# Twenty more transposing jobs of a two-block transformer step move from TensorE to VectorE's 32x32 squares and on-chip transfers

## The chip, the cores and the metric

One core of one Trainium2 chip runs the whole program. The metric is the device time of one execution in microseconds (us). Lower is better.

## What is computed

The reference runs three layers one after the other on 256 tokens of width 2048, all in float32: a pooling mixer, a sparse attention whose keys an indexer picks, and a block with an mLSTM branch, a MoBA attention branch and a feed-forward part. Almost all of the work is in products of the tokens with weight matrices. Between them stand norms, rotations and attention.

```
h = rms_norm(x, g) * (1 + scale) + shift              # twice, one per mixer
out = (mixed * silu(gate)) @ w_out                    # pooling
q, k, v, gate, qi, ki, wi = split(h @ w_in)           # q, k: 8 blocks of 512 columns
out = (sparse_attention(rope(q), rope(k), v, picked by qi, ki, wi) * silu(gate)) @ w_out
x = rms_norm(x + gate * out, final_g)
mq, mk, mv, mo, mi, mf, aq, ak, av, g_m, g_a = split(rmsnorm(x, w) @ w_in_2)
mq, mk = silu(causal_depthwise_conv([mq, mk], 4 taps))
merged = sigmoid(g_m) * (h_m @ w_m) + sigmoid(g_a) * (h_a @ w_a)
x = x + rmsnorm(merged @ w_out_2);   x = x + rmsnorm(relu(norm(x) @ w_up)**2 @ w_down)
```

## The kernel before, in words

**The product.** Everything that is multiplied by weights goes through one pipeline. A weight matrix of 2048 rows is read in *blocks* of 512 columns, and each block in 8 *chunks* of 256 rows (512 KB). SyncE loads a chunk into one of 8 buffers `raw`. ScalarE rounds it to the short float32r form (`hi`, L524), VectorE subtracts that from the original (`lo`, L1057), and TensorE then multiplies in three passes, so that the sum has nearly the precision of float32: tokens-hi by weights-hi, tokens-hi by weights-lo, tokens-lo by weights-hi (L1924 to L1926). A chunk is 12 matmuls of 128x512. `w_hi` and `w_lo` have 4 buffers each, so ScalarE can start on chunk n only when TensorE is through with chunk n-4, and the two engines run at most about three chunks ahead. How long a chunk's `lo` is finished before TensorE starts it is called its *lead* here.

**The order of the work** is written out by hand for each engine. `blk` walks over the chunks from 3 to 10 (0 to 2 of the next block included), and *hooks* hang other work behind a chunk: `{5: f}` runs `f` after chunk 5 of this walk, `{2: f}` before the first of it. At the end of a block ScalarE empties PSUM into `stage` (`evac`, L536 and L532), and VectorE does there what the block needs (rotations of q and k, gating, residual sums). Nothing lets an engine run its own list in another order.

**The transposing jobs.** The products have tokens on the partitions, but the next product or the attention needs features there. So a block's 256 tokens by 512 features in `stage` are transposed. TensorE does this in a *job*: 8 transposes of 128x128 (L1994) into two PSUM banks, hung behind chunk 3 of the next block. VectorE then takes the result out of PSUM (`leave`, L1139 and L1141, hook 5), ScalarE rounds it to `hi` where it is the token side of a product (`split`, L563), and VectorE subtracts (`low_part`, L1149). The 4 causal taps of the convolution (`conv`, L1594 and L1597, hooks 7 to 10) read their job's PSUM banks directly.

**The other way** exists already in the feed-forward part. There VectorE transposes the 32x32 squares of `stage` into `blocks` in one instruction (L1845), GpSimd issues 16 transfers of 32 partitions by 1 KB each, from SBUF to SBUF, which bring the squares to their partitions in `gathered` (L510), and ScalarE and VectorE take them from there (L989). A transposed block with its 16 transfers is called a *turn* below, its 16 transfers a *cross*, and the instruction that reads `gathered` the *taker*.

**Stages** in order, with their blocks of weights: `qk` (8 blocks), `gate` (4), `v` (4), attention, `attn_out` (4), `m_qk` (4), `m_v` (2), `m_o` (2), mLSTM, `a_qk` (4), `a_v` (2), MoBA, `g_m` (4), `g_a` (4), `branch` (4), `mix_out` (4), feed-forward (32). In `gate`, *riders* go along: VectorE adds up 512 KB pieces of `mod_w` beside the weights (L1300), one for each chunk, with a load of their own each. The jobs are named after the stage or norm they serve: `qk` (8), `norm2` (4, in `attn_out`), `m_qk` (4), `a_qk` (4), `branch` (4). The last job of one stage falls in the first block of the next. Between `m_qk` and `m_v` stands `m_if`, a product of 8 columns, whose result TensorE transposes back in `if_back` (L2292), behind chunk 0 of the second block of `m_v`.

GpSimd's queue also carries the large transfers: the residual to DRAM and back (2 MB each), the rows that are spread over all partitions (`final_g`, `gate_row` and others, 1 MB each). It works in order.

## Time and profile before

| | us |
|---|---|
| median of 3 runs (2375.24 to 2379.03) | 2377.76 |
| the profiled execution | 2376.75 |
| its span, first to last instruction | 2374.9 |
| TensorE busy (98%) | 2326.1 |
| VectorE busy (64%) | 1528.7 |
| ScalarE busy (47%) | 1117.7 |
| GpSimd busy (6%) | 140.4 |
| one block of 96 matmuls without anything between them | 21.76 |

Execution time and span differ by what lies around the first and last instruction. Matmuls are pipelined in the profile, so the starts of two of them, and not their durations, tell how long TensorE needs for one. A busy share is an average over stages that differ: what a change is worth is read where it stands, from which wait ends last.

### The profile page before, as it was taken

The page shows a single profiled execution, that of the slowest core. Times are in us where ns is not written, and L with a number is a line of the kernel's source. Part 1 is how long each engine was busy: PE and PEld are TensorE (multiplying, and loading weights), DVE is VectorE, ACT ScalarE, POOL GpSimd, SP SyncE. Part 2 cuts the span into 40 slices and gives each one's busy share as a digit, 9 for nine tenths or more (in the row PEclk, how much of TensorE's full clock was granted, in tenths as well). Part 3 has the DMA queues.
Part 4 walks back from the last instruction along what each step waited for, and adds up shares of the span by engine and source line. Part 5 has one row for each costly group of instructions (what it writes and reads, how often), then busy time and mean ns, then how long its engine had stood idle before and what let it go on. Part 6 is the DMA issues. An engine that isn't in the chain of part 4 may idle for free.

```text
span 2374.9 us, 30018 instructions
## 1 busy us (share of the span) xinstructions
PE 2326.1 (98%) x10902; PEld 1888.6 (80%) x10902; DVE 1528.7 (64%) x1863; ACT 1117.7 (47%) x1347; POOL 140.4 (6%) x277
## 2 busy tenths in 40 slices
PE   5999999999999999999999999999999999999998
PEld 1877777888788878888888888888888888888886
DVE  2988887666697556875765444665665665565566
ACT  1444445444444455545444444454554444454454
POOL 0000000000000000000000000000131121121120
PEclk8999999999999999999999999999999999999999
DMA  9999996555597546656454766556566666666663
GB/s 392 386 377 378 376 398 250 181 178 176 191 382 268 169 157 196 224 160 188 133 185 151 238 193 190 179 198 196 177 213 208 201 211 204 203 209 195 209 208 110
DMA packets 253414, 536.59 MB, mean 226 GB/s; under 512 B 25068, under 2 KB 25332, under 8 KB 249336
## 3 DMA queue, kind: packets, MB, share of 16 engines
q1 hardware_dynamic: 241520, 510.40, 63.6%
q0 software_dynamic: 10128, 22.07, 2.7%
q10 hardware_dynamic: 1656, 2.65, 0.3%
q8 instruction: 69, 1.13, 0.2%
q14 instruction: 41, 0.34, 0.0%
HBM read 520.35 MB, written 6.30 MB: 222 GB/s over the span
## 4 chain that ended last, share of the span: by engine, by line
PE 93%; DVE 3%; DMA 2%; ACT 1%; issue 1%; ACTq 0%; DVEq 0%; SPq 0%
PE ps L1924 29%; PE ps L1926 29%; PE ps L1925 29%; PE ps L1994 2%; DMA ifb<-in_f_bias 1%; PE ps L2024 1%; PE ps L2203 0%; DMA T<-in_mod_w 0%; DVE w_lo L1057 0%; PE ps L2244 0%; PE ps L2103 0%; PE ps L2180 0%; ACT tmp L807 0%; PE ps L2246 0%; PE ps L2245 0%
## 5 line engine op out<-in xcount | busy, mean ns | idle before, releaser
L1057 DVE TENSOR_TENSOR w_lo<-raw,w_hi 128x1024 fp32r<-128x1024 f32 x784 | 944.9, 1217 | 527.9 <-ACT w_hi L524 513.5
L524 ACT CAST w_hi<-raw 128x1024 fp32r<-128x1024 f32 x784 | 815.7, 1046 | 875.0 <-PE ps L1926 827.5
L1924 PE MATMUL ps<-w_hi,xa_hi 128*128 128x512 f32 x2176 | 855.4, 393 | 5.3 <-DVE w_lo L1057 3.1
L1926 PE MATMUL ps<-w_hi,xa_lo 128*128 128x512 f32 x2176 | 847.5, 389 | 0.0
L1925 PE MATMUL ps<-w_lo,xa_hi 128*128 128x512 f32 x2176 | 846.9, 389 | 0.0
L1924 PEld LDWEIGHTS ps<-w_hi,xa_hi 128*128 128x128 f32 x2176 | 408.6, 188 | 99.5 <-issue 11.0
L1926 PEld LDWEIGHTS ps<-w_hi,xa_lo 128*128 128x128 f32 x2176 | 408.5, 188 | 85.9
L1925 PEld LDWEIGHTS ps<-w_lo,xa_hi 128*128 128x128 f32 x2176 | 408.7, 188 | 82.6
L1924 PE MATMUL ps<-w_hi,xb_hi 128*128 128x512 f32 x928 | 364.6, 393 | 2.0 <-issue 1.3
L1926 PE MATMUL ps<-w_hi,xb_lo 128*128 128x512 f32 x928 | 361.4, 389 | 0.0
L1925 PE MATMUL ps<-w_lo,xb_hi 128*128 128x512 f32 x928 | 361.2, 389 | 0.0
L1924 PEld LDWEIGHTS ps<-w_hi,xb_hi 128*128 128x128 f32 x928 | 174.2, 188 | 45.9 <-issue 9.2
L1926 PEld LDWEIGHTS ps<-w_hi,xb_lo 128*128 128x128 f32 x928 | 174.2, 188 | 36.5
L1925 PEld LDWEIGHTS ps<-w_lo,xb_hi 128*128 128x128 f32 x928 | 174.3, 188 | 35.2
L510 POOL DMA_DIRECT2D T<-T x256 | 125.2, 497 | 512.8 <-DVE T L1845 451.8
L536 ACT ACTIVATE stage<-ps 128x1024 f32<-128x1024 f32 (+1 forms) x60 | 61.6, 1026 | 85.9 <-PE ps L1926 85.9
L1300 DVE SCALAR_TENSOR_TENSOR T<-T,csil 128x1024 f32<-128x1024 f32 x64 | 81.9, 1280 | 9.3 <-DMA T<-in_mod_w 7.4
L1300 DVE SCALAR_TENSOR_TENSOR wide<-T,csil,wide 128x1024 f32<-128x1024 f32 x64 | 81.9, 1279 | 0.5 <-DVE stage L1236 0.4
L2024 PE MATMUL ps<-T,csil 128*32 128x256 f32 (+1 forms) x384 | 45.4, 549 | 21.2 <-DMA T<-in_mod_w 21.1
L1880 DVE TENSOR_TENSOR T<-T,stage 128x1024 f32<-128x1024 f32 x27 | 33.1, 1225 | 32.6 <-ACT stage L536 32.5
L2024 PEld LDWEIGHTS ps<-T,csil 128*32 128x32 f32 x384 | 8.1, 114 | 48.4 <-DMA T<-in_mod_w 27.2
L1139 DVE COPY T<-ps 128x1024 f32 (+1 forms) x14 | 17.1, 1224 | 40.2 <-PE ps L1994 40.2
(266 smaller groups left out, 1046.9 us busy)
## 6 DMA issues: line engine op xcount, KB each, us to landing
raw<-in_w_in SPq DMA_DIRECT2D x176, 512.0 KB, 3.9
T<-in_mod_w SPq DMA_DIRECT2D x160, 512.0 KB, 7.7
raw<-in_attn_w_in SPq DMA_DIRECT2D x144, 512.0 KB, 4.5
raw<-in_w_up SPq DMA_DIRECT2D x128, 512.0 KB, 4.2
raw<-in_w_down SPq DMA_DIRECT2D x128, 512.0 KB, 4.5
raw<-in_pool_w_in SPq DMA_DIRECT2D x64, 512.0 KB, 8.0
T<-in_mod_w SPq DMA_DIRECT2D x16, 1024.0 KB, 8.9
raw<-in_pool_w_out SPq DMA_DIRECT2D x32, 512.0 KB, 8.9
```

What stands on the lines that cost most here:

```text
L510: pool.dma_start(gathered[32 * f:32 * f + 32, a, :, :], blocks[32 * a:32 * a + 32, f, :, :]).then_inc(blocks_landed, 16)
L524: nc.scalar.copy(w_hi[:, o % SPL, :, 0:cols], raw[:, o % RAW, :, 0:cols]).then_inc(hi_ready, 1)
L536: nc.scalar.activation(dst, ps[:, bass.ds((A % 2) * 2, 2), :], func).then_inc(acc_free, 1)
L1057: tt(w_lo[:, o % SPL, :, part], raw[:, o % RAW, :, part], w_hi[:, o % SPL, :, part].bitcast(F32), ALU.subtract).then_inc(lo_ready, 1)
L1139: nc.vector.tensor_copy(dst, src).then_inc(tp_evac, 1)
L1300: stt(acc, ride_raw[:, o % 4, :], csil[:, bass.ds(b * 4 + o // 2, 1)], acc, ALU.mult, ALU.add).then_inc(mod_used, 1)
L1880: tt(y, y, stage[:], ALU.add).then_inc(combined, 1)
L1924: mm(dst, x_hi, h, start=first and k == 0, stop=False)
L1925: mm(dst, x_hi, l, start=False, stop=False)
L1926: ins = mm(dst, x_lo, h, start=False, stop=last and k == KPC - 1)
L1994: ins = nc.tensor.transpose(dst, part, ident)
L2024: ins = mm(ps[32 * q:32 * q + 32, bank, at:at + n], col, src[:, q * n:q * n + n], start=first, stop=k == KC - 1, skip_group_check=True)
```

## The change

Twenty of TensorE's jobs become turns: 8 of `qk`, 3 of `norm2`, 2 of `m_qk` (blocks 0 and 1 of its 4), 4 of `a_qk`, 3 of `branch`. The last job of `norm2` and of `branch`, and the last two of `m_qk`, stay on TensorE. The table of jobs is cut, and a table of turns is new:

```diff
-        ("idx_kw", 2, False), ("qk", 8, False), ("attn", 4, True), ("norm2", 4, True), ("m_qk", 4, False), ("m_if", 1, False),
-        ("mlstm", 2, True), ("a_qk", 4, False), ("moba", 2, True), ("branch", 4, True), ("norm3", 4, True),
+        ("idx_kw", 2, False), ("qk", 0, False), ("attn", 4, True), ("norm2", 1, True), ("m_qk", 2, False), ("m_if", 1, False),
+        ("mlstm", 2, True), ("a_qk", 0, False), ("moba", 2, True), ("branch", 1, True), ("norm3", 4, True),
...
+    for name, jobs in (("qk", 8), ("norm2", 3), ("m_qk", 2), ("a_qk", 4), ("branch", 3)):
```

GpSimd gets the crosses, between its large transfers. From the second turn of a group on, a cross also waits until the taker before it has read `gathered`:

```diff
+            def cross(src, dst, landed):
+                for a in range(4):
+                    for f in range(4):
+                        pool.dma_start(dst[32 * f:32 * f + 32, a, :, :], src[32 * a:32 * a + 32, f, :, :]).then_inc(landed, 16)
+            def turns(name, jobs, src, dst, taken, first=0):
+                for b in range(jobs):
+                    pool.wait_ge(turn_ready, TURNS[name] + b + 1)
+                    if b:
+                        pool.wait_ge(taken, first + b)
+                    cross(src, dst, turn_landed)
...
+            turns("qk", 8, blocks, gathered, unfolded)
...
             widen(gate_row)
+            turns("norm2", 3, blocks, gathered, xh_ready, SPLITS["norm2"])
             pool.wait_ge(res_done, 1)
             pool.dma_start(tokens(resid[1]), T2[:]).then_inc(res_stored, 16)
+            turns("m_qk", 2, blocks3, gathered3, unfolded, 8)
+            turns("a_qk", 4, blocks3, gathered3, unfolded, 10)
...
+            turns("branch", 3, blocks, gathered, x_ready, SPLITS["branch"])
```

VectorE's transpose, and the places where it stands. In `qk` it follows the rotation, ahead of the next block's first `lo`; in `norm2` it stands behind chunk 3; in `m_qk` ahead of chunk 3; in `a_qk` where `leave` stood; in `branch` ahead of chunk 3:

```diff
+            def turn_blocks(dst, done):
+                nc.vector.transpose(dst.rearrange("p f q i -> p q f i"),
+                                    stage[:].rearrange("p t (f c i) -> p (t f) c i", c=4, i=32)).then_inc(done, 1)
+            def turn(name, b, dst):
+                if TURNS[name] or not (isinstance(b, int) and b == 0):
+                    dve.wait_ge(turn_landed, b * 256 + TURNS[name] * 256)
+                turn_blocks(dst, turn_ready)
...
-                blk(b + B0, {3: lambda: qi_out_now(b), 5: lambda: qk_out(b - 1), 9: lambda: index_scores(b)})
+                blk(b + B0, {3: lambda: qi_out_now(b), 9: lambda: index_scores(b)})
                 query_key(b, b + A0)
+                qk_turn(b)
...
-            phase("gate", first={5: lambda: qk_out(7)})
+            phase("gate")
...
+            with step.loop(2, n, 2) as b:
+                blk(b + B0, {3: lambda: norm_turn(b - 1), 5: lambda: norm_low(b - 2)})
...
-                blk(b + B0, {7 + f: (lambda f=f: conv(b - 1, f)) for f in range(4)})
+                blk(b + B0, {1: {2: lambda: conv_turn(0)}, 2: {2: lambda: conv_turn(1), **convs(0, 3)},
+                             3: {**convs(1, 3), **convs(2, 7)}}[b])
...
             def aqk_out(b):
-                leave(b + JOBS["a_qk"], feat(2)[:, bass.ds(b * 4, 4), :])
+                turn("a_qk", b, blocks3)
...
+                if not first:
+                    dve.wait_ge(staged, b + STAGED["branch"])
+                    turn("branch", b - 1, blocks)
```

The takers are ScalarE's, each one block later than the job's `leave` was. `unfold` copies `gathered` to where the attention or the convolution reads it. `norm2_split` scales four strips by the norm's weights into `tmp` and rounds them; `split_gathered` only rounds:

```diff
+            def unfold(name, b, src, dst):
+                act.wait_ge(*turned(name, b))
+                nc.scalar.copy(dst.rearrange("p f (t a i) -> p f t a i", t=NT, a=4),
+                               src.rearrange("p a (t f) i -> p f t a i", t=NT)).then_inc(unfolded, 1)
...
+            with act.Fori(2, n) as b:
+                blk(b + B0, {2: lambda: qk_unfold(b - 2), 8: lambda: index_relu(b)})
...
+                blk(B0 + b, {2: lambda: qk_unfold(6 + b)} if b < 2 else None)
...
+                blk(B0 + b, {**({2: lambda: norm2_split(b - 2)} if b > 1 else {}), 6: lambda: attn_squares(b - 1)})
...
+                    {}, {2: lambda: conv_unfold(0), 8: lambda: conv_silu(0)},
+                    {2: lambda: conv_unfold(1), 7: lambda: conv_silu(1)})):
...
+                blk(B0 + b, {4: lambda: aqk_unfold(b - 2)} if b > 1 else None)
...
+                    if o == 3 and not isinstance(b, int):
+                        split_gathered(*turned("branch", b - 2), XB, b - 2)
```

TensorE loses the jobs. The two convolution jobs that stay use one PSUM bank pair, which `if_back` uses too, so its wait now covers the last of the convolutions:

```diff
-                blk(b + B0, b + A0, XB, True, {3: lambda: qk_job(b - 1), 5: lambda: index_scores(b)})
-            phase("gate", XB, first={3: lambda: qk_job(7)})
+                blk(b + B0, b + A0, XB, True, {5: lambda: index_scores(b)})
+            phase("gate", XB)
...
+            def conv_job(b):
+                job(b + (JOBS["m_qk"] - 2), stage, acc_free, PHASES["m_qk"][1] + b + 1, bank=4)
...
             def if_back():
                 pe.wait_ge(acc_free, PHASES["m_if"][1] + 1)
-                pe.wait_ge(tp_evac, JOBS["m_if"] - 1)
+                pe.wait_ge(tp_evac, JOBS["m_if"])
```

How VectorE's instructions stand at two places. First, the end of the last `qk` block and the start of `gate`, before (`COPY stage<-tmp` ends the rotation, `wide<-T,csil,wide` is a rider, `w_lo` is the `lo` of a chunk, `T<-ps` is `leave`):

```order
L1236 COPY stage<-tmp 128x8x16 [waits dve_step]
L167 REGISTER_ALU
L173 REGISTER_ALU [waits dve_step]
L173 COMPARE_AND_BRANCH
L1300 SCALAR_TENSOR_TENSOR wide<-T,csil,wide 128x1024 [waits ride_landed0,bias_landed]
L1300 SCALAR_TENSOR_TENSOR wide<-T,csil,wide 128x1024 [waits ride_landed1,mod_used]
L1300 SCALAR_TENSOR_TENSOR wide<-T,csil,wide 128x1024 [waits ride_landed2,mod_used]
L1057 TENSOR_TENSOR w_lo<-raw,w_hi 128x1024 [waits hi_ready,mod_used]
```

and now:

```order
L1353 COPY stage<-tmp 128x8x16 [waits dve_step]
L180 REGISTER_ALU
L1256 STREAM_TRANSPOSE T<-stage 128x8x4x32 [waits dve_step,turn_landed]
L186 REGISTER_ALU
L186 COMPARE_AND_BRANCH
L1417 SCALAR_TENSOR_TENSOR wide<-T,csil,wide 128x1024 [waits ride_landed0,bias_landed]
L1417 SCALAR_TENSOR_TENSOR wide<-T,csil,wide 128x1024 [waits ride_landed1,mod_used]
L1417 SCALAR_TENSOR_TENSOR wide<-T,csil,wide 128x1024 [waits ride_landed2,mod_used]
L1158 TENSOR_TENSOR w_lo<-raw,w_hi 128x1024 [waits hi_ready,mod_used]
```

The transpose has come between the rotation and the three riders that stand ahead of chunk 3 of `gate`; the `leave` two chunks further on is gone.

Second, the end of block 0 of `m_qk` and the start of its block 1, before (`T<-T,small` is the first output of a token tile, `if_lo` the low part of the gates' weights):

```order
L1578 SCALAR_TENSOR_TENSOR T<-T,small 128x2048
L1057 TENSOR_TENSOR w_lo<-raw,w_hi 128x1024 [waits hi_ready,dve_step]
L1578 SCALAR_TENSOR_TENSOR T<-T,small 128x2048
L1605 TENSOR_TENSOR if_lo<-if_raw,if_hi 128x128 [waits dve_step,if_high]
L1057 TENSOR_TENSOR w_lo<-raw,w_hi 128x1024 [waits hi_ready] x5
L1594 TENSOR_SCALAR tmp<-ps,vec 128x256 [waits tp_ready]
L1597 SCALAR_TENSOR_TENSOR tmp<-ps,vec,tmp 128x253 [waits dve_step]
```

and now:

```order
L1709 SCALAR_TENSOR_TENSOR T<-T,small 128x2048
L1158 TENSOR_TENSOR w_lo<-raw,w_hi 128x1024 [waits hi_ready,dve_step]
L1709 SCALAR_TENSOR_TENSOR T<-T,small 128x2048
L1746 TENSOR_TENSOR if_lo<-if_raw,if_hi 128x128 [waits dve_step,if_high]
L1256 STREAM_TRANSPOSE T<-stage 128x8x4x32 [waits turn_landed,acc_free]
L1158 TENSOR_TENSOR w_lo<-raw,w_hi 128x1024 [waits hi_ready] x8
L1256 STREAM_TRANSPOSE T<-stage 128x8x4x32 [waits turn_landed,acc_free]
```

A transpose has come ahead of chunk 3 of block 1, and the first convolution has left that block: it stands in block 2, behind the second transpose.

## Rows read from the trace of the kernel before

**Rows 1.** The page, busy time of each engine, and the chain that ended last.
```profile
PE 2326.1 (98%) x10902; PEld 1888.6 (80%) x10902; DVE 1528.7 (64%) x1863; ACT 1117.7 (47%) x1347; POOL 140.4 (6%) x277
...
PE 93%; DVE 3%; DMA 2%; ACT 1%; issue 1%; ACTq 0%; DVEq 0%; SPq 0%
```

**Rows 2.** Timeline of TensorE at a `qk` job: start us, duration us, instruction.
```profile
510.51 0.39 PE L1926 MATMUL ps<-w_hi,xa_lo 128*128 128x512 f32 x1
510.74 1.03 PE L1994 MATMUL ps<-con,stage 128*128 128x128 f32 x8
511.53 0.48 PE L1924 MATMUL ps<-w_hi,xa_hi 128*128 128x512 f32 x1
```

**Rows 3.** Groups by form: busy us, mean ns of one | idle before.
```profile
L1845 DVE STREAM_TRANSPOSE T<-stage 128x1024 f32<-128x1024 f32 x16 | 19.9, 1246 | 0.5
...
L989 ACT CAST xa_hi<-T 128x1024 fp32r<-128x1024 f32 x16 | 16.8, 1049 | 9.5 <-DMA T<-T 9.5
...
L1139 DVE COPY T<-ps 128x1024 f32 x10 | 12.2, 1224 | 33.2 <-PE ps L1994 33.2
```

**Rows 4.** Timeline of VectorE in block 3 of `qk`: `lo` of chunk 3.
```profile
527.85 1.23 DVE L1057 TENSOR_TENSOR w_lo<-raw,w_hi 128x1024 fp32r<-128x1024 f32 x1 [0.65 <-ACT w_hi L524]
```

**Rows 5.** TensorE starting chunk 3 (`qk` 3, `gate` 0, `attn_out` 3, `m_qk` 1), then `if_back`.
```profile
531.76 0.39 PE L1924 MATMUL ps<-w_hi,xa_hi 128*128 128x512 f32 x1
...
651.68 0.50 PE L1924 MATMUL ps<-w_hi,xa_hi 128*128 128x512 f32 x1 [0.93 <-DVE w_lo L1057]
...
932.81 0.39 PE L1924 MATMUL ps<-w_hi,xb_hi 128*128 128x512 f32 x1
...
978.15 0.39 PE L1924 MATMUL ps<-w_hi,xa_hi 128*128 128x512 f32 x1
...
1069.06 0.29 PE L2292 MATMUL ps<-con,stage 8*128 8x8 f32 x2
```

**Rows 6.** Timeline of VectorE at the start of `gate`.
```profile
646.44 3.93 DVE L1300 SCALAR_TENSOR_TENSOR wide<-T,csil,wide 128x1024 f32<-128x1024 f32 x3 [0.39 <-DVE stage L1236]
650.40 1.22 DVE L1057 TENSOR_TENSOR w_lo<-raw,w_hi 128x1024 fp32r<-128x1024 f32 x1
```

**Rows 7.** Timeline of VectorE where block 1 of `m_qk` begins.
```profile
976.51 0.29 DVE L1605 TENSOR_TENSOR if_lo<-if_raw,if_hi 128x128 fp32r<-128x128 f32 x1 [0.16 <-DVE T L1578]
976.72 4.62 DVE L1057 TENSOR_TENSOR w_lo<-raw,w_hi 128x1024 fp32r<-128x1024 f32 x4
```

**Rows 8.** Timeline of VectorE in `m_v`: the last taps of the last convolution.
```profile
1068.38 1.52 DVE L1597 SCALAR_TENSOR_TENSOR tmp<-ps,vec,tmp 128x253 f32<-128x253 f32 x3
```

**Rows 9.** Timelines of ScalarE (end of a block) and VectorE in `attn_out` 3.
```profile
925.01 1.03 ACT L536 ACTIVATE stage<-ps 128x1024 f32 x1 [1.83 <-PE ps L1926]
...
930.04 3.49 DVE L1057 TENSOR_TENSOR w_lo<-raw,w_hi 128x1024 fp32r<-128x1024 f32 x3
```

**Rows 10.** Crosses of the feed-forward part: VectorE, GpSimd and ScalarE timelines, GpSimd's waits.
```profile
1735.53 1.25 DVE L1845 STREAM_TRANSPOSE T<-stage 128x1024 f32<-128x1024 f32 x1
...
1747.98 2.93 POOL L510 DMA_DIRECT2D T<-T  x6 [5.85 <-issue]
...
1824.08 7.82 POOL L510 DMA_DIRECT2D T<-T  x16 [51.21 <-DVE T L1845]
...
1754.24 1.05 ACT L989 CAST xa_hi<-T 128x1024 fp32r<-128x1024 f32 x1 [1.26 <-DMA T<-T]
...
POOL T L510 <- issue: 60.9, 13, 6.3
```

**Rows 11.** Stretches of 23 and 22 us in `qk` and `gate`: ..., clock, DMA share, GB/s.
```profile
476.00:499.00 23.00, 23.00 (x111) 18.66 (x110) 15.83 (x25) 10.18 (x12) 0.00 (x0) 1.00 0.57 186
...
666.00:688.00 22.00, 22.00 (x99) 18.23 (x98) 20.93 (x19) 9.72 (x10) 0.00 (x0) 1.00 1.02 385
```

**Rows 12.** Timelines of GpSimd and VectorE around the start of `attn_out`.
```profile
872.97 0.54 POOL L465 DMA_DIRECT2D wide<-gate_row  x1 [11.93 <-DMA T<-in_final_g]
...
881.23 1.22 DVE L1377 TENSOR_TENSOR stage<-stage,wide 128x1024 f32<-128x1024 f32 x1 [2.08 <-DMA wide<-gate_row]
```

More of the change, by code:

```diff
@@ L126, in _jobs @@
         JOBS[name], SPLITS[name] = n, s
-        n, s = n + jobs, s + (4 if name == "shift0" else jobs if split else 0)
+        n, s = n + jobs, s + (4 if name in ("shift0", "norm2", "branch") else jobs if split else 0)
 _jobs()
@@ L507, in _ @@
                 pool.wait_ge(blocks_ready, n + 1)
[L508 to L511 removed]
+                cross(blocks, gathered, blocks_landed)
         @block.scalar
@@ L1774, in _ @@
             branch(0, first=True)
-            with step.loop(1, n, 2) as b:
+            branch(1)
+            with step.loop(2, n, 2) as b:
                 branch(b)
@@ L2351, in _, with branch @@
             B0, A0, n = PHASES["branch"]
[L2352 to L2354 removed]
+            def branch(b):
                 for half in range(2):
```

228 lines of the change are left out of this document (139 added, 89 removed).

## The prediction, made before the changed kernel ran

> **What bounds the kernel now.** I read four views, in this order. The page says which engine ends the program: TensorE is busy for 98% of the span, and 93% of the chain that ended last is TensorE's own work; the other engines have a third to a half of their time free on average [rows 1]. So every TensorE instruction that goes away shortens the program, as long as what replaces it arrives in time on engines with room. The timeline of TensorE gives the price of a job. The job's first transpose starts at 510.74 in the ordinary step of 0.23 us behind the last product, and the next product starts at 511.53 [rows 2]. A job costs 0.79 us.
>
> The average hides where the other engines have no room. The place that matters is chunk 3 of each block: ScalarE's emptying of PSUM and VectorE's end-of-block work both stand ahead of it, while TensorE has only three finished chunks, 8.2 us, to live on. So the third view is that chunk's lead, VectorE's timeline against TensorE's. It is 531.76 - 529.08 = 2.7 us in the middle of `qk` [rows 4, 5]. In block 1 of `m_qk` it is 0.2: the first of four `lo` that begin at 976.72 ends near 977.95, TensorE starts at 978.15 [rows 5, 7]. At the start of `gate` there is none, TensorE already idles 0.93 us for it [rows 5, 6]. The fourth view is how long a cross takes, read in the feed-forward part.
>
> **The change part by part.**
>
> *TensorE.* Twenty jobs at 0.79 us leave: **-15.8 us**. All stood behind chunk 3 of a block full of products, and nothing but products moves up.
>
> *VectorE.* Each turn is one transpose of 1.25 us where `leave` took 1.22 [rows 3]. The amount is the same; the place is not.
> - `qk`: `leave` stood at hook 5, the transpose stands ahead of chunk 3. It takes 1.25 of a lead of 2.7 and leaves 1.4. Cost 0; in block 1, where the engine came late from the indexer's first block, I allow 0 to 0.3.
> - `gate`, block 0: the same transpose stands ahead of three riders that together take 3.93 us and a `lo` that TensorE already waits for [rows 5, 6]. Everything is in series there: **+1.2**.
> - `m_qk`, block 1: the transpose stands ahead of the `lo` with a lead of 0.2 [rows 7]. 1.25 - 0.2: **+1.0**. The engine runs without a break there, so nothing absorbs it. The convolutions that move to blocks 2 and 3 make VectorE lose 0.55 us a chunk against TensorE (1.22 for `lo` and about 2.05 for a strip, against 2.72), over four and then eight chunks. They start from some 3 us of lead, and the eight-column product of `m_if` gives 5.5 us back behind them: 0, at most 1.
> - `attn_out`, `a_qk`, `branch`: the transpose is off the path. In `a_qk` it stands exactly where `leave` did; in `branch` it takes 1.25 of some 3 us of lead.
>
> *`if_back`.* It now waits for the last taps of the last convolution. They end at 1068.38 + 1.52 = 1069.90 [rows 8], and the transposes started at 1069.06 [rows 5]: 0.84 and a semaphore, **+0.9**.
>
> *ScalarE* gets 14 copies that it did not have, 1.05 us each [rows 3]. The three takers of `branch` replace a `split` of the same size; those of `norm2` grow from 1.05 to about 3.0 (four quarter strips of about 0.5 in front). With 8 `hi` and an emptying it uses about 10 of 23 us a block in `qk` [rows 11], so the work fits. What matters is when the cross has landed, since ScalarE, and every `hi` behind it, stands still until then. The shortest possible cross is 16 issues in 7.82 us and some 4 us more; but GpSimd often pauses in the middle, 5.85 us in one case, 13 times in 256 issues [rows 10]. So most crosses hold a pause. A paused one ran from the transpose's end at 1736.78 to its taker at 1754.24, 17.5 us, and ScalarE waited 1.26 for it [rows 10].
> - `qk`: the block of rows 4 starts at 531.76 - 8.16 = 523.6, and the transpose would end 4.9 us into it. A block will last 22.95 us, and ScalarE has emptied it 1.4 us after its end (926.04 in a block that starts at 932.81 - 8.16 = 924.65 [rows 5, 9]). From transpose to taker there are 19.4 us; ScalarE has 1.4 us more before it delays VectorE, and the lead is 1.4: safe up to 22 us. Cost 0.
> - `norm2`: the `lo` begins at 930.04, the transpose follows and ends near 932.5. ScalarE is free for the taker when it has emptied the next block, 21.76 us after 926.04 [rows 9], so 15.3 us later. A cross of 17.5 makes it 2.2 late. Then 3.0 for the taker, 1.05 for `hi` and 1.2 for `lo` end 7.45 after the emptying, at 933.5 in this block's frame, and TensorE wants the chunk at 932.81 [rows 5]: 0.7 late. Only a pause near the end of a cross does this. I count one of three: **+0.7**, 0 to 2.1.
> - `m_qk`, `a_qk`, `branch`: the takers are up to 2.5 us late as well, but at hooks 3 and 4, or with 2 us in hand: 0.
>
> *GpSimd and the transfers.* 320 issues at 0.49 us are 157 us in a queue that is busy for 6% now. A cross moves 0.5 MB beside a weight stream that uses 57% of the DMA engines in `qk`: room. In `gate` the share is 1.02, 385 GB/s [rows 11], and the last cross of `qk` falls there: 0 to 1.4 us if the loads have to make way (0.5 MB at that rate). I take 0, since the lead grows through that stage and the removed `leave` gives VectorE 1.2 back.
>
> **Sum:** -15.8 + 1.2 + 1.0 + 0.9 + 0.7 = -12.0. The profiled execution took 2376.75 and the median of the runs is 1.0 above it, so 2377.76 - 12.0 = **2366 us**. Below 0.2% (4.8 us) a measurement of this kernel can hardly tell a difference from none.
>
> **The rivals.**
>
> *A, everything hidden.* No transpose and no taker costs TensorE anything; then it is 2377.8 - 15.8 = 2362. For it: the large leads in most blocks. Against it: three of the four costs stand in unbroken series in the trace. Chance 0.09.
>
> *B, crosses held up by large transfers and full DMA engines.* If a pause means that GpSimd waits for whatever is under way, it is longer behind a large transfer. `gate_row` took from 872.97 to about 881.2, and VectorE idled 2.08 us for it [rows 12]; were the load ahead of it held up by the reload of the residual, the first residual sum would be 1 to 3 us later, with a lead of 1.4 there. The first cross of `m_qk` comes right behind a store of 2 MB. With `gate` slowed by up to 1.4, this adds 1 to 5 us: 2369. Chance 0.15. The Trainium skill ("DMA: Bandwidth & Descriptors", the section on the descriptor swizzle) counts 9 descriptors per DMA engine for a 128-partition transfer of 1 MiB, 8 of data and one of completion. By that count a transfer of 32 partitions needs 3, and the pauses would come from a full list of descriptors, at places that the large transfers shift; the trace fits in that unpaused and paused crosses alternate irregularly, and no row shows a pause behind a large transfer.
>
> *C, the freed time comes back as waits.* If the next chunk 3 were VectorE's to decide in most stages, TensorE would wait there for what it saved. In `a_qk` it already waits about 0.1 us a block. But that wait is measured from the start of a block, and the job stood behind the chunk, so it doesn't grow. The result would be within 5 us of before: 2374. Chance 0.07.
>
> *D, slower: crosses that take 20 us.* The windows are 15.3 us plus 1.5 of lead in `norm2`, about 18 in `a_qk`, 22 in `qk`. At 20 us each, `norm2` loses 3 x 3.2, `a_qk` 4 x 1.8, `branch` and `m_qk` some 3 more: 2366 + 19 = 2385. It is slower than before from about 19 us on. For it: the longest of the feed-forward part is 17.5, only 1.5 less, and there the taker stands 16 us behind the transpose. Against it: the 16 issues take 0.49 us each, evenly, while VectorE works beside them [rows 10], and these stages load the DMA engines no more than that one does. Chance 0.05, with all other causes of a slower run. The Trainium skill ("SBUF — State Buffer", the section on who interferes with whom) says that GpSimd can't write a transfer's descriptors while VectorE runs a float32 copy inside SBUF: such a transfer goes from some 620 to 3100 ns. The rotations of `qk` and `a_qk` end in such a copy, of 0.2 to 0.4 us. If it held up all 16 issues fivefold, a cross would take over 40 us, by that estimate far slower than before; a single short copy can delay one issue. Of that the feed-forward rows show nothing.
>
> **The numbers.** The sum's way has 0.64, A 0.09, B 0.15, C 0.07, D 0.05. The range goes from A's value less the scatter of a median to B's far end, 2361.5 to 2373. Faster by over 0.2% are the sum, A and B, 0.88; within it is C, 0.07; slower is D, 0.05.
>
> **What would show it.** 160 transposes fewer: TensorE's L1994 group with source `stage` falls from 288 to 128. TensorE's idle at chunk 3 of `gate` 0 grows from 0.93 to about 2.1; a new one of 1.0 stands in `m_qk` 1; `if_back` waits for a convolution for 0.9. In `attn_out` ScalarE waits for a cross before at most two takers, and no other taker delays TensorE. All `qk` blocks get shorter by 0.8. I am wrong if waits of ScalarE for `gathered` stand ahead of waits of TensorE in `qk` or `a_qk`, if `gate` is longer by over 2 us, or if GpSimd's pauses are much longer than 6 us.

## The result, and the profile after

| | before | changed |
|---|---|---|
| median of 4 runs (us) | 2377.49 (2375.24 to 2379.03) | 2363.07 (2362.46 to 2365.53) |
| ratio, 95% interval | | 0.9946 (0.9934 to 0.9958) |
| the profiled execution, its span | 2376.75, 2374.9 | 2362.46, 2360.7 |

The changed kernel is 14.4 us faster, 0.5%; 2366 was predicted, in a range of 2361.5 to 2373. The page of the changed kernel, busy time and chain, against [rows 1]:

```profile
PE 2310.7 (98%) x10742; PEld 1872.0 (79%) x10742; DVE 1531.1 (65%) x1868; ACT 1134.5 (48%) x1373; POOL 297.3 (13%) x597
...
PE 89%; DVE 4%; ACT 2%; DMA 2%; issue 2%; POOL 1%; ACTq 0%; DVEq 0%
```

TensorE lost exactly 160 instructions, 20 jobs of 8. ScalarE and GpSimd took up the takers and the crosses. GpSimd is for the first time in the chain that ended last, with 1%.

**Where the time went, block by block.** A block's length is the time from its first product to the next block's. Not all of the 14.2 us between the two spans is the change's. TensorE's timeline at the first product of `qk`, before and after:

```profile
452.65 0.47 PE L1924 MATMUL ps<-w_hi,xa_hi 128*128 128x512 f32 x1
```

```profile
451.28 0.47 PE L2056 MATMUL ps<-w_hi,xa_hi 128*128 128x512 f32 x1
```

Up to there the change moves no instruction, and the changed run is 1.37 us ahead. The profiles of all runs scatter there, from 451.1 to 453.6 (see e7), so I count this as chance. From there to the end of the span it is 2374.9 - 452.65 = 1922.25 before and 2360.7 - 451.28 = 1909.42 after: **-12.8 us**. The block lengths give the same. A name like `qk` 3 stands for block 3 of that stage, counted from 0:

| blocks | before | changed | difference |
|---|---|---|---|
| 18 blocks that only lost their job | 22.65 to 24.01 each | 21.76 to 23.09 | -16.6 |
| `gate` 0 (lost a job) | 23.88 | 25.45 | +1.6 |
| `m_qk` 0 (keeps its job) | 22.69 | 23.17 | +0.5 |
| `m_qk` 1 (lost a job) | 22.65 | 23.51 | +0.9 |
| `m_v` 1 (`if_back`) | 22.89 | 23.91 | +1.0 |
| all others (mainly a wait in the attention behind `v` 3) | | | -0.2 |

**A job was worth 0.92, not 0.79.** Each of the 18 blocks got shorter by 0.87 to 1.02, most by 0.89 or 0.93. The product behind a job starts 0.79 after the first transpose [rows 2], but the next product starts 0.31 behind that one, where the ordinary step is 0.23. This is its row in the kernel before, behind the last of rows 2 (511.53):

```profile
511.84 0.40 PE L1925 MATMUL ps<-w_lo,xa_hi 128*128 128x512 f32 x1
```

That makes 0.87. The rest, up to 0.06, is in the next few steps, each some ns longer than usual.

**The gate.** VectorE's timeline in the changed kernel, then TensorE's, against [rows 5, 6]:

```profile
638.48 1.25 DVE L1256 STREAM_TRANSPOSE T<-stage 128x1024 f32<-128x1024 f32 x1
639.65 3.88 DVE L1417 SCALAR_TENSOR_TENSOR wide<-T,csil,wide 128x1024 f32<-128x1024 f32 x3
643.57 1.22 DVE L1158 TENSOR_TENSOR w_lo<-raw,w_hi 128x1024 fp32r<-128x1024 f32 x1
```

```profile
644.85 0.50 PE L2056 MATMUL ps<-w_hi,xa_hi 128*128 128x512 f32 x1 [1.80 <-DVE w_lo L1158]
...
645.88 0.45 PE L2057 MATMUL ps<-w_lo,xa_hi 128*128 128x512 f32 x1
646.12 0.63 PE L2058 MATMUL ps<-w_hi,xa_lo 128*128 128x512 f32 x1
...
649.52 0.39 PE L2057 MATMUL ps<-w_lo,xa_hi 128*128 128x512 f32 x1
```

The wait grew from 0.93 to 1.80, as foreseen in kind. The rest was not foreseen: 1.2 us behind the wait, eight steps in a row take 0.43 in place of 0.23. The stretches around it (columns: us, PE, PEld, DVE, ACT and POOL busy, granted clock, DMA share, GB/s) name the cause:

```profile
642.66:644.85 2.19, 0.39 (x3) 0.01 (x1) 2.15 (x3) 1.05 (x1) 2.19 (x5) 1.00 0.96 328
644.85:646.10 1.25, 1.25 (x5) 1.04 (x6) 1.22 (x2) 0.00 (x0) 1.25 (x4) 0.99 0.94 331
646.10:649.50 3.40, 3.40 (x9) 2.63 (x8) 3.37 (x3) 0.10 (x1) 0.77 (x2) 0.50 1.05 342
```

For 3.4 us the granted clock is 0.50, that is 1.2 for 2.4 GHz: 8 x 0.20 = 1.6 us. Gross, with the lost job put back, the block costs 2.5: 0.9 of wait and 1.6 of clock.

**The late cross.** GpSimd's and ScalarE's timelines in `norm2` (second and third turn):

```profile
902.33 2.46 POOL L494 DMA_DIRECT2D T<-T  x5 [12.61 <-DVE T L1256]
909.20 5.37 POOL L494 DMA_DIRECT2D T<-T  x11 [4.41 <-issue]
925.47 4.88 POOL L494 DMA_DIRECT2D T<-T  x10 [10.90 <-DVE T L1256]
935.09 2.94 POOL L494 DMA_DIRECT2D T<-T  x6 [4.74 <-issue]
```

```profile
919.02 1.71 ACT L925 ACTIVATE tmp<-T,vec 128x256 f32<-128x256 f32 x4 [1.30 <-DMA T<-T]
941.21 1.71 ACT L925 ACTIVATE tmp<-T,vec 128x256 f32<-128x256 f32 x4 [1.73 <-DMA T<-T]
```

Two crosses in a row hold a pause of over 4 us. The first makes its taker 1.3 late, so the next transpose comes late as well, and the third taker is 1.7 late. The loss falls in `m_qk` 0 and 1. There TensorE waits for chunk 3 behind the transpose, and in `m_v` for the convolution:

```profile
971.13 0.50 PE L2056 MATMUL ps<-w_hi,xa_hi 128*128 128x512 f32 x1 [1.45 <-DVE w_lo L1158]
...
1061.40 0.25 PE L2423 MATMUL ps<-con,stage 8*128 8x8 f32 x2 [0.98 <-DVEq L1733]
```

### The profile page after: what moved, and what is told of

It reads as the page before. It is cut to its first block, busy times and chain, and to the rows that moved or that the text cites. A ratio compares the mean times of both kernels' runs of the same rounds, so it can differ in the third digit from the quotient of the medians.

```text
span 2360.7 us, 29885 instructions
## 1 busy us (share of the span) xinstructions
PE 2310.7 (98%) x10742; PEld 1872.0 (79%) x10742; DVE 1531.1 (65%) x1868; ACT 1134.5 (48%) x1373; POOL 297.3 (13%) x597
## 4 chain that ended last, share of the span: by engine, by line
PE 89%; DVE 4%; ACT 2%; DMA 2%; issue 2%; POOL 1%; ACTq 0%; DVEq 0%
PE ps L2056 28%; PE ps L2058 28%; PE ps L2057 28%; DMA ifb<-in_f_bias 1%; PE ps L2126 1%; PE ps L2156 1%; DVE w_lo L1158 1%; POOL T L494 1%; PE ps L2335 1%; ACT w_hi L563 0%; DMA T<-T 0%; PE ps L2376 0%; PE ps L2235 0%; PE ps L2312 0%; ACT tmp L880 0%
## 5 line engine op out<-in xcount | busy, mean ns | idle before, releaser
L494 POOL DMA_DIRECT2D T<-T x576 | 282.0, 498 | 1186.0 <-DVE T L1256 1031.0
L1256 DVE STREAM_TRANSPOSE T<-stage 128x1024 f32<-128x1024 f32 x36 | 44.8, 1244 | 3.8 <-ACT stage L571 1.7
```

Source lines behind the costliest of these rows:

```text
L494: pool.dma_start(dst[32 * f:32 * f + 32, a, :, :], src[32 * a:32 * a + 32, f, :, :]).then_inc(landed, 16)
L1256: nc.vector.transpose(dst.rearrange("p f q i -> p q f i"), stage[:].rearrange("p t (f c i) -> p (t f) c i", c=4, i=32)).then_inc(done, 1)
```

## The experiments

Each is the changed kernel with the edit shown, and was profiled once beside the kernel before on the same chip; three were also timed in five runs. A single run's total says little about 1 or 2 us: the head of the program ahead of `qk`, where no instruction is edited, ended at 451.3 in the changed kernel's profile and at 453.0 and 453.4 in those of two variants. Most block lengths repeat to 0.05 us from profile to profile, and they decide. Four don't: `attn_out` 1 and 3 and `m_qk` 0 and 1 vary by up to 0.7 even where nothing in them was edited, so a difference there in a single profile shows little.

### e1_gate_late: the transpose out of the gate's first chunks

```diff
-            with step.loop(1, n, 11) as b:
+            with step.loop(1, n - 1, 11) as b:
...
+            blk(B0 + n - 1, {3: lambda: qi_out_now(n - 1), 9: lambda: index_scores(n - 1)})
+            query_key(n - 1, A0 + n - 1)
...
-            phase("gate")
+            phase("gate", first={5: lambda: qk_turn(7)})
...
-                blk(B0 + b, {2: lambda: qk_unfold(6 + b)} if b < 2 else None)
+                blk(B0 + b, {2: lambda: qk_unfold(6 + b // 2)} if b in (0, 2) else None)
```

> The eighth transpose of qk stands behind chunk 5 of the first gate block, where leave stood before, and its taker in the third gate block. Theory (the transpose in series with the riders makes TensorE wait, and the longer wait sets the clock to half for 3.4 us): block 0 of gate falls from 25.45 us to 22.9 to 23.1, TensorE's wait at chunk 3 from 1.80 to 0.6, and no stretch with a granted clock of half there; the whole 2.5 us shorter. Rival (the clock fell for another reason than the wait): the block falls by 1.2 only, to 24.2, and the half clock stays. Second rival (the cross falls between full DMA engines and is late for the third block): ScalarE waits before its taker there and the third gate block gets longer than 21.76.

Measured: 2360.67. `gate` 0 is 23.13, and no half clock:

```profile
644.68 0.50 PE L2058 MATMUL ps<-w_hi,xa_hi 128*128 128x512 f32 x1 [0.75 <-DVE w_lo L1158]
```

```profile
644.68:648.00 3.32, 3.32 (x15) 2.74 (x16) 3.29 (x3) 0.60 (x2) 0.00 (x0) 1.00 0.92 329
```

The block gets the whole 2.3 back; the third gate block stays at 21.76. Neither rival holds. Not all of it reaches the end, though: the last block of `v` with the attention behind it lasts 57.74 here for 57.45 in the changed kernel, 0.3 more. It does so in all three profiles that have this edit (e1, e7, e10) and in no other of the changed kernel's variants; before it was 57.69. There one wait of TensorE for ScalarE is 1.08 in place of 0.80. Why it depends on this edit isn't shown. The net gain is 2.0.

### e2_gate_warm and e6_warm8: TensorE busy while it waits

The diff is e2's; e6 has 8 for 16.

```diff
+            def warm():
+                for _ in range(16):
+                    mm(ps[:, 5, 0:P], ident, ident, start=True, stop=True)
...
-            phase("gate", XB)
+            phase("gate", XB, first={2: warm})
```

> As the changed kernel, with 16 matmuls of 128x128 into an unused PSUM bank ahead of chunk 3 of the first gate block, which fill about 1.8 us of TensorE's wait there. The sum is the same: no useful work is moved. Theory (idle time of TensorE makes the clock fall): no half clock behind it, the block falls from 25.45 to 23.9 to 24.1. Rival (the clock falls with what VectorE, the transfers or power do there, or on its own): the half clock stays and the block stays at 25.4 or gets longer.

> As e2_gate_warm, with 8 matmuls in place of 16: there one took 0.21 us, so 16 filled 3.5 us where the wait was 2.0, and the 1.5 us too many hid what the clock gave back. Eight end about when chunk 3 is ready. Theory: no half clock behind them, block 0 of gate 23.9 to 24.1 for 25.45 in the changed kernel. Rival (the block is as long whatever TensorE does in the wait): 25.3 or more again.

Measured: 2361.13 and 2363.13. TensorE's timeline of e2, then of e6:

```profile
642.68 3.73 PE L2327 MATMUL ps<-con 128*128 128x128 f32 x32
646.17 0.48 PE L2056 MATMUL ps<-w_hi,xa_hi 128*128 128x512 f32 x1
```

```profile
645.23 1.95 PE L2327 MATMUL ps<-con 128*128 128x128 f32 x16
647.19 0.50 PE L2056 MATMUL ps<-w_hi,xa_hi 128*128 128x512 f32 x1
```

The number for e2 was missed: its block is 25.35. A matmul of 128x128 float32 shows as two instructions and takes 0.22 us here, and 16 of them last 3.5 us where 2.0 were free. The half clock was gone all the same. With 8 the wait is as long as in the changed kernel (chunk 3 starts 1.96 beyond its step) and the block is 23.85, 1.6 shorter, with no more useful work done:

```profile
646.40:650.00 3.60, 3.58 (x19) 2.94 (x19) 3.57 (x4) 0.12 (x1) 2.79 (x6) 1.00 1.04 345
```

VectorE and the DMA engines are as busy as in the half-clock stretch. So at this place it is TensorE's idle time that brings the clock down, and neither its neighbours nor chance does. The half clock stood in `gate` 0 in every profile with the transpose ahead of the riders and nothing in the wait (the changed kernel, e3, e4, e5, e8, e9, e11 and, with a longer wait, e12), in none of before, e1, e2, e6, e7 and e10. It began 0.5 to 1.5 us behind the end of the wait, which was 1.80 in all seven, and in e12 within a wait of 4.04.

The length of the wait alone doesn't decide, as e12 (below) shows: there TensorE once waits 2.80 in `attn_out` 3 and the clock stays up, while behind one of 2.48 in `mix_out` 0 it falls. The row of the first wait and the stretch behind it:

```profile
945.02 0.50 PE L2064 MATMUL ps<-w_hi,xb_hi 128*128 128x512 f32 x1 [2.80 <-DVE w_lo L1166]
```

```profile
945.00:948.50 3.50, 3.48 (x15) 2.88 (x16) 3.50 (x4) 3.44 (x7) 2.09 (x5) 1.00 0.59 158
```

What else decides stays open.

### e3_conv_if: two costs apart from each other

```diff
-                blk(b + B0, {1: {2: lambda: conv_turn(0)}, 2: {2: lambda: conv_turn(1), **convs(0, 3)},
+                blk(b + B0, {1: {3: lambda: conv_turn(0)}, 2: {2: lambda: conv_turn(1), **convs(0, 3)},
...
-                u = ps[:, 4 + f // 2, f % 2 * S:f % 2 * S + S] if b >= 2 else conv_u[:, f, :]
+                u = ps[:, 2 * b + f // 2, f % 2 * S:f % 2 * S + S] if b >= 2 else conv_u[:, f, :]
...
-                job(b + (JOBS["m_qk"] - 2), stage, acc_free, PHASES["m_qk"][1] + b + 1, bank=4)
+                job(b + (JOBS["m_qk"] - 2), stage, acc_free, PHASES["m_qk"][1] + b + 1, bank=2 * b)
...
-                pe.wait_ge(tp_evac, JOBS["m_if"])
+                pe.wait_ge(tp_evac, JOBS["m_if"] - 1)
```

> Two edits at places that don't touch: the first transpose of m_qk moves from ahead of chunk 3 to behind it, and the last convolution's job takes the other pair of PSUM banks, so that if_back waits only for the convolution before it. Theory: m_qk block 1 falls from 23.51 by 1.25 to 22.2 to 22.4 (0.4 of its gap stays, from norm2's late cross), m_v block 1 from 23.91 to 22.9; together 2.2 to 2.3 us shorter. Rival for m_qk (VectorE is behind anyway, the wait only moves to the next chunk): it falls by less than 0.4. Rival for if_back (something else of the same length ends its wait, such as the emptying of m_if's bank): m_v block 1 stays at 23.9.

Measured: 2360.87; `m_qk` 1 is 22.39, `m_v` 1 is 22.89. VectorE's timeline at block 1 of `m_qk`, then TensorE's there and at `if_back`:

```profile
969.28 1.22 DVE L1158 TENSOR_TENSOR w_lo<-raw,w_hi 128x1024 fp32r<-128x1024 f32 x1
970.42 1.24 DVE L1256 STREAM_TRANSPOSE T<-stage 128x1024 f32<-128x1024 f32 x1
971.58 4.59 DVE L1158 TENSOR_TENSOR w_lo<-raw,w_hi 128x1024 fp32r<-128x1024 f32 x4
```

```profile
970.55 0.50 PE L2056 MATMUL ps<-w_hi,xa_hi 128*128 128x512 f32 x1 [0.32 <-DVE w_lo L1158]
...
1059.79 0.29 PE L2423 MATMUL ps<-con,stage 8*128 8x8 f32 x2
```

The `lo` goes first, the wait falls from 1.45 to 0.32, and `if_back` doesn't wait at all. Both costs are what the prediction said they are, each repaired where it stands.

### e4_ring: twice the space for descriptors

```diff
-    nc = bacc.Bacc("TRN2", target_bir_lowering=False, num_devices=1, dynamic_dma_scratch_size=1024)
+    nc = bacc.Bacc("TRN2", target_bir_lowering=False, num_devices=1, dynamic_dma_scratch_size=2048)
```

> As the changed kernel, with twice the space for the descriptors of GpSimd's transfers (2048 bytes a partition for 1024). Theory (GpSimd stops after every 21st issue of 32 partitions since its list of descriptors is full): the pauses go from 29 to about 14 in the turns and come after every 42nd issue; if none falls into the third cross of norm2, ScalarE's wait of 1.73 us before that taker goes and m_qk block 0 falls from 23.17 to 22.7, block 1 by about 0.4 too. Rival (a pause is a wait for the DMA engines or for a fixed number of transfers under way): still 29 pauses after every 21st, of 6.2 us, and the same times.

Measured: 2362.13. GpSimd's waits of the changed kernel, and of e4 (its turns and the feed-forward crosses together: us in total, times, longest):

```profile
POOL T L494 <- issue: 128.2, 29, 6.2
```

```profile
POOL T L494 <- issue: 64.5, 16, 6.8
```

In an unbroken series of crosses a pause came behind every 21st issue with 1024 bytes, and behind every 42nd with 2048; behind the store of 2 MB in `m_qk`, with 1024 bytes, it came after 9 issues and then after 12. So the pauses follow the space for descriptors, and the rival is out. The Trainium skill ("DMA: Bandwidth & Descriptors", the section on the descriptor swizzle) counts 8 descriptors of data and one of completion for each DMA engine in a transfer over 128 partitions. My estimate from that is 2 and one for 32 partitions, and it agrees with the trace if 1024 bytes hold 64 of them: 64 / 3 = 21. GpSimd's timeline of e4 in `norm2`:

```profile
902.77 7.83 POOL L494 DMA_DIRECT2D T<-T  x16 [12.15 <-DVE T L1256]
924.84 4.88 POOL L494 DMA_DIRECT2D T<-T  x10 [14.24 <-DVE T L1256]
934.16 2.94 POOL L494 DMA_DIRECT2D T<-T  x6 [4.44 <-issue]
```

The third cross still pauses; the second doesn't. ScalarE's wait before the third taker falls from 1.73 to 0.96, `m_qk` 0 from 23.17 to 22.69, `m_qk` 1 by 0.3. That these times are the larger space's doing isn't shown: e1, e2 and e5 pause at the same issues as the changed kernel, ScalarE waits 0.4 at most there, and their `m_qk` 0 is 22.69 and `m_qk` 1 22.85 to 22.87 as well. `attn_out` 1 got 0.6 longer (22.33), since `gate_row` landed later in that run (VectorE waited 3.81 for it); see e10.

### e5_price: what a job costs

```diff
+            def again(n):
+                for i in range(n):
+                    ins = nc.tensor.transpose(ps[:, 5, i % 4 * P:i % 4 * P + P], ident, ident)
...
-                blk(b + B0, b + A0, XB, True, {5: lambda: index_scores(b)})
-            phase("gate", XB)
+                blk(b + B0, b + A0, XB, True, {3: lambda: again(8), 5: lambda: index_scores(b)})
+            phase("gate", XB, lambda b: again(16))
```

> As the changed kernel, with 8 transposes of a constant into an unused PSUM bank behind chunk 3 of qk blocks 1 to 7, where the jobs stood, and 16 behind chunk 3 of gate blocks 1 to 3. The output isn't touched. Theory (a job costs what the block lengths say, since the product behind it starts late too): qk blocks 2 to 7 grow from 22.85 by 0.90 to 0.93, gate blocks 1 and 2 from 21.76 by 1.7 to 1.8. Rival (the price read from the starts holds, 0.79 for eight, and the rest of the saving was slack that came back): they grow by 0.79 and 1.6.

Measured: 2374.45, and `qk` 2 to 7 are 23.75 or 23.78, 0.90 and 0.93 more than in the changed kernel; `gate` 1 and 2 are 23.53 and 23.56, 1.77 and 1.80 more. So eight transposes cost 0.92 and eight more 0.87, and the rival with 0.79 is out.

### e7_joined: all repairs

The edits of e1, e3 and e4, and:

```diff
+            def pads(at, n):
+                for i in range(at, at + n):
+                    pool.dma_start(pad[0:32, i:i + 1], con[32:64, i:i + 1]).then_inc(padded, 16)
...
             widen(gate_row)
+            pads(0, 10)
```

> All repairs at once: e1_gate_late, both edits of e3_conv_if, the larger descriptor space of e4_ring, and ten transfers of 128 bytes behind gate_row, in time that GpSimd waits anyway, which shift the full list from the middle of the third cross of norm2 (there after 10 of 16 issues) to its start. Theory (the list counts issues, 42 at this size): all three crosses of norm2 run without a pause, ScalarE doesn't wait for any, m_qk block 0 is 22.69; block 1 is 21.8 to 22.2, gate block 0 23.1, m_v block 1 22.9. Sum against the changed kernel: -2.3 -0.5 -1.5 -1.0 = -5.3 (-4.5 to -6), so 2357 to 2358.5. Rival (the costs are one another's cover, or the pause comes where it likes): the third cross still pauses, or less than 3 us is gained in all.

Measured in five runs: 2360.52 (2359.23 to 2361.15), ratio to before 0.9934 (0.9920 to 0.9947); 2.1 us less than the changed kernel on the same chip (e9), where 4.5 to 6 were expected. The blocks are as forecast: `gate` 0 23.13, `m_qk` 0 22.69, `m_qk` 1 22.03, `m_v` 1 22.89. From the first product of `qk` on the span is 2357.4 - 453.03 = 1904.4, against 1909.4 of the changed kernel: 5.0 less. The 0.3 that is missing to the forecast 5.3 is the longer wait in the attention (e1). What is missing in the profiled run's total lies ahead of `qk`, where this run took 1.7 longer than the changed kernel's. The granted clock goes with it: ahead of `qk` it is at half for 27.3 us in e7, 27.3 in e10 and 30.7 in e6, the three slowest heads (453.0 to 453.6), and for 6.8 to 23.9 us in all others. e6 has none of e7's edits, so this looks like scatter. Of the five runs of e7 the profiled one was the fastest, 3.4 under the profiled run of e9. By the medians the rival's "less than 3 us" came true, by the blocks it didn't, and its other half did. The pause didn't move:

```profile
867.71 4.95 POOL L500 DMA_DIRECT2D pad<-con  x10
...
924.44 4.90 POOL L496 DMA_DIRECT2D T<-T  x10 [14.47 <-DVE T L1263]
934.41 2.94 POOL L496 DMA_DIRECT2D T<-T  x6 [5.07 <-issue]
```

### e9_changed_again: what repeats

> The changed kernel once more, as the base of the others on this chip: 2362 to 2364, ratio to before 0.9935 to 0.9955. If the third cross of norm2 is late by the pause's place alone, m_qk block 0 is 23.1 to 23.2 and block 1 23.4 to 23.6 again; if it was chance, block 0 is 22.69 and block 1 22.8 to 23.2, as in e1 and e2.

Measured in five runs: 2362.60 (2361.52 to 2363.39), ratio 0.9942 (0.9928 to 0.9955). `gate` 0 is 25.50 with its half clock, `m_qk` 1 23.49, `m_v` 1 23.97. `m_qk` 0 is 22.65, but `attn_out` 3 is 22.19 for 21.76: the second cross was 2.1 late here and cost 0.4 one block earlier. This matches neither half of the expectation. In eight profiles with 1024 bytes and unedited crosses in `norm2` (the changed kernel, e1, e2, e3, e5, e6, e9, e11) the pauses stand behind the same issues, 3.9 to 5.5 us long. In five of them the second and third takers are both late, by 0.8 to 2.1, in the other three by 0.4 at most. So the place of a pause is fixed, and whether it costs 1.1 us, as in the first profile, or nothing is chance.

### e11_shift: another attempt to move the pause

```diff
+            def pads():
+                for i in range(5):
+                    if i == 4:
+                        pool.wait_ge(padded, 64)
+                    at = i % 4 * 32
+                    pool.dma_start(pad[at:at + 32, :], con[32:64, 0:256]).then_inc(padded, 16)
...
             widen(gate_row)
+            pads()
```

> The changed kernel (1024 bytes for the descriptors, a pause after every 21st issue of a series) with five more transfers behind gate_row, of 32 partitions by 1 KB each like those of a cross, into a tensor that nothing reads. The ten of 128 bytes in e7_joined had not moved the pause. Theory (what counts is the size: small transfers take no room in the list): the count starts with these five, so 5 + 16 are through before the second cross of norm2, which runs without a pause or with one ahead of its first issue, and the third pauses after 5 issues for 10. Rival (the count starts anew with the first cross behind a large transfer, whatever lies between): pauses after 5 issues of the second and after 10 of the third, as without them.

Measured: 2363.28; the pauses stand behind 5 issues of the second cross and 10 of the third, as without the five. The rival holds: in e7 and here, what was issued between a large transfer and a series' first cross didn't count. Why, stays open; in both cases over 4 us passed between the last of these transfers and the cross, and no run tried it without that.

### e8_late_cross and e12_later_cross: how far the cliff is

The *cliff* is the length of a cross from which its taker delays TensorE. The diff is e8's; e12 issues 18 ahead of each cross, into a smaller tensor over all partitions.

```diff
+            def pads(at, n):
+                for i in range(at, at + n):
+                    pool.dma_start(pad[0:32, i:i + 1], con[32:64, i:i + 1]).then_inc(padded, 16)
...
+                    pads(8 * (TURNS[name] + b), 8)
                     cross(src, dst, turn_landed)
```

> The changed kernel with every one of the 20 crosses made later: GpSimd issues 8 transfers of 128 bytes ahead of it (0.495 us each, so 4.0 us). The longest crosses then take 20 to 21.5 us from the transpose to the taker, rival D's case. My windows (22 us in qk, 18 in a_qk, 15.3 and 1.5 in norm2): qk loses 0 to 0.5 a block, norm2 some 3 us for each of its three crosses, a_qk 1 to 2 for each, m_qk and branch 3 to 6 together; the program 2373 to 2390. D as it was priced says 2385. If the crosses are off the path (the room in the queues is larger than I read it), it stays within 4 us of 2362.6.

> As e8_late_cross, with 18 small transfers ahead of each cross (8.9 us). In e8 the crosses held no pause of 4 to 6 us any more, so they lasted 16 us, as long as the paused ones of the changed kernel, and the case of 20 us was not reached. Here 0.3 + 8.9 + 7.8 and some 3.5 to land make 20.5 us, without pauses. Theory (rival D's arithmetic, windows of 22 in qk, 18 in a_qk, 15.3 and 1.5 in norm2): qk still loses nothing; each cross of norm2 3 to 4 us, each of a_qk 1.5 to 3, m_qk and branch 3 to 8 together; the program 2376 to 2392. Rival (the takers have more room than I read, or a late one only moves waits that are there anyway): below 2370. With pauses on top, the program is above 2392.

e8 measured 2364.11, against my 2373 to 2390: the small transfers took the long pauses away. GpSimd's timeline of e8 in `norm2`:

```profile
926.11 2.45 POOL L500 DMA_DIRECT2D pad<-con  x5 [11.43 <-DVE T L1263]
928.76 1.47 POOL L500 DMA_DIRECT2D pad<-con  x3 [0.21 <-issue]
930.23 7.82 POOL L496 DMA_DIRECT2D T<-T  x16
```

A stop of 0.21 in place of 4 to 6 us; in `m_qk` the stops are up to 0.76. From first issue to taker (942.31) it is 16.2, while the changed kernel's paused third cross has 941.21 - 925.47 = 15.7. So e8 tests crosses that are all as long as the paused ones, and that costs 1.8 us in the blocks (`attn_out` 3 +0.3, `m_qk` 0 +0.8, `m_qk` 2 +0.65); of this single profile some may be scatter. It didn't reach 20 us.

e12 did: 2422.19, **60 us slower** than the changed kernel and 47 slower than before. Here pauses are back, of 1 to 4.5 us, in each of the 20 crosses behind the 21st issue counted from its first small transfer. GpSimd in `attn_out` 2, ScalarE, and TensorE in `qk` 3:

```profile
918.94 2.44 POOL L501 DMA_DIRECT2D pad<-con  x5 [8.54 <-DVE T L1264]
921.59 6.36 POOL L501 DMA_DIRECT2D pad<-con  x13 [0.21 <-issue]
927.95 1.47 POOL L496 DMA_DIRECT2D T<-T  x3
932.05 6.37 POOL L496 DMA_DIRECT2D T<-T  x13 [2.63 <-issue]
```

```profile
939.98 1.71 ACT L933 ACTIVATE tmp<-T,vec 128x256 f32<-128x256 f32 x4 [4.79 <-DMA T<-T]
```

```profile
531.80 0.50 PE L2064 MATMUL ps<-w_hi,xa_hi 128*128 128x512 f32 x1 [1.14 <-DVE w_lo L1166]
```

From first issue to taker there are 21.0 us, in the other crosses 20 to 24 (25 in `gate`), and ScalarE waits up to 10.7 for them (`a_qk`). By stage, against the changed kernel: `qk` +7.3 (1.0 to 1.4 a block), `gate` +3.1, `attn_out` 2 to `m_qk` 0 +17, the rest of `m_qk` +7.6, `a_qk` and `a_v` +14, `branch` and `mix_out` +10. A part of that is clock: from `gate` on, in and behind the waits, the granted clock is 0.50 in eight stretches, 41 us together, where the changed kernel has one of 3.4. In `qk`, where the crosses take 22 to 23 us against my window of 22, nothing of that kind occurs and each block loses little. Rival D was right in kind, and its 19 us for crosses of 20 were too few for these: a taker that is late also holds back the next cross and, since the transpose waits for the last cross to land, VectorE.

### e10_rows_first: `final_g` ahead of the large reload

e7 without the ten small transfers, and on GpSimd:

```diff
-            pool.dma_start(T0[:], tokens(resid[0])).then_inc(res_landed, 16)
             pool.wait_ge(o_done, DSA_HEADS)
             pool.wait_ge(row_stored, 64)
             widen(final_g.rearrange("(a n) -> a n", a=1), final_w)
+            pool.dma_start(T0[:], tokens(resid[0])).then_inc(res_landed, 16)
```

> As e7_joined without the ten small transfers, and with final_g's transfer ahead of the residual's reload of 2 MB instead of behind it. GpSimd waits for final_g to land before it issues gate_row, 12 to 13 us in every run so far, and VectorE waits for gate_row (2.8 to 3.8 us in the changed kernel's runs and their variants, 2.1 before), which leaves chunk 3 of attn_out 1 a lead of 0.05 to 0.65. Theory (final_g lands late since it stands behind the reload): GpSimd's wait falls to 3 to 6 us, VectorE's to below 1, the lead of that chunk is over 2, the transpose of each norm2 turn comes earlier in its block, and m_qk block 1 is 21.8 to 22.0. It gains 0.3 to 0.8 on e7_joined: 2359 to 2360.5. Rival (the row takes its 12 us anyway, being spread over 128 partitions): same waits, same time as e7_joined.

Measured in five runs: **2358.08** (2356.94 to 2359.37), ratio to before 0.9914 (0.9901 to 0.9928), the lowest of all and below the 2359 to 2360.5 that I expected. GpSimd's row of `gate_row` in the changed kernel, then in e10, and VectorE's first residual sum in each:

```profile
867.83 0.54 POOL L488 DMA_DIRECT2D wide<-gate_row  x1 [13.14 <-DMA T<-in_final_g]
```

```profile
864.83 0.55 POOL L488 DMA_DIRECT2D wide<-gate_row  x1 [9.04 <-DVE xb_lo L1184]
```

```profile
875.54 1.22 DVE L1494 TENSOR_TENSOR stage<-stage,wide 128x1024 f32<-128x1024 f32 x1 [2.79 <-DMA wide<-gate_row]
```

```profile
874.27 1.23 DVE L1494 TENSOR_TENSOR stage<-stage,wide 128x1024 f32<-128x1024 f32 x1 [1.48 <-ACT stage L575]
```

GpSimd still waits 9.0, not 3 to 6, but now for VectorE, which has to be through with what `wide` held. `gate_row` is issued 3 us earlier, and VectorE waits for ScalarE alone. Chunk 3 of `attn_out` 1 has a lead of 1.96, and `m_qk` 1 is 21.87. The profiled run's span from `qk` on is 2357.6 - 453.37 = 1904.2, as in e7 (1904.4). So the swap itself bought 0.2 (`m_qk` 1), below the forecast 0.3 to 0.8; the 2.4 us between the medians of e7 and e10, which come from two chips, are not shown to be its doing.

## Why the prediction was right, and where it was off

The sum was -12.0 and the blocks say -12.8. The other 1.6 of the measured 14.4 are not the change's as far as the profiles show: they have 1.4 of it ahead of `qk`.

- **TensorE, -15.8:** this term was mis-sized. The 20 jobs gave back 18 x 0.92 = 16.6 and 2 x 0.92 inside `gate` 0 and `m_qk` 1, 18.4 together. I took the price from one start to the next and left out that the product behind a job is followed late, 0.31 for 0.23, and the next ones by some ns each. e5 put the jobs back and measured 0.90 to 0.93.
- **`gate` 0, +1.2:** right in place, wrong in size, 2.5, and the larger part of it by a mechanism that the working didn't have. The wait grew by 0.9, since 0.39 of idle time ahead of the riders [rows 6] took up a part. Behind it the clock fell, 1.6 us (e1, e2, e6). "`gate` longer by over 2 us", which I had named as a sign that I was wrong, was so in gross terms (the block itself, which lost a job, grew by 1.6); nothing in the working had a clock in it.
- **`m_qk` 1, +1.0:** right. Without late takers in `norm2` the block is 22.87 (e1), 1.1 over 21.76, and e3 moves the transpose and gets it back.
- **`if_back`, +0.9:** right, 0.98 of wait and 1.0 in the block; e3.
- **`norm2`, +0.7:** right in mechanism, a pause near the end of a cross. But two takers were late, not one of three, for the pauses come behind a fixed number of issues and a late taker delays the next transpose. It cost 0.5 in `m_qk` 0 (or, in e9, in `attn_out` 3) and 0.6 more in `m_qk` 1 (23.51 against e1's 22.87): 1.1. In e2 and e5 it cost nothing, so the forecast 0.7 lies inside a scatter from 0 to 1.1.
- **Costs set to nothing:** right. `qk` blocks 2 to 7 keep a lead of 2.0 at chunk 3 and each is exactly one job shorter; `a_qk` waits no longer than before (the step to chunk 3 is 1.18 over the ordinary one in block 1 both before and after, then 0.01 for 0.11); `branch` keeps 1.8. In `a_qk` and `branch` takers of ScalarE waited up to 1.8 and TensorE didn't feel it; in `qk` none waited.

So terms of opposite sign were both too small: 2.6 too little gain, 1.9 too little cost (5.7 for 3.8). The total was nearer than its parts deserved, and that is luck: a right count of jobs and right places, with two errors that offset each other. The measured 2363.1 is even nearer rival A's 2362 than the sum's 2366; only the blocks tell them apart.

**Rivals.** A (all hidden) is refuted by three repairs, e1 and both of e3, that each gave time back. B (late behind large transfers, full DMA engines): VectorE's wait for `gate_row` grew from 2.08 to between 2.2 and 3.8, which cost nothing or up to 0.6 in `attn_out` 1; `gate` behind block 0 lost nothing, and the pause in the cross behind the 2 MB store, 2.7 us, was shorter than most. C didn't occur: 18 blocks got shorter by the full price of a job, 0.87 to 1.02. D didn't occur, and none of the changed kernel's 576 issues of 32 KB took longer than 0.63 us. But e12 shows its cliff: in e8 crosses of some 16 us cost 2, in e12 crosses of 20 to 24 cost 60. I had it at 0.05 on a margin of 1.5 us in `norm2`, which proved thin but real. (Its parts add up to 19.8, not 19; nothing hangs on that.)

## What to carry to other kernels

Price an instruction group by the length of the block with and without it, not by the step to the next instruction alone. When work is added ahead of an instruction that the bound engine already waits for, ask what else hangs on the length of that wait: here a wait that doubled cost more in clock than in waiting, and moving one transpose behind chunk 5 gave 2.3 us in its block. For a transfer that replaces an engine's work, the window from its start to its taker decides everything; measure the transfer with its pauses, and stretch it on purpose once to see how far the cliff is.
